# Two matmuls for each pair of weight halves instead of three: a 512-column moving tile, slabs of 256 columns

## The reference, cut to what matters

```python
proj = rms_norm(h) @ w_in              # 2048 x 9216, then attention, a 31-tap convolution, gates
y_attn = attention(q, k, v) @ w_attn_o # 1024 x 2048
y_conv = conv(...) @ w_conv_o          # 1024 x 2048
h = h + rms_norm(merged @ w_out)       # 2048 x 2048
gate, up = split(rms_norm(h) @ w_gate_up)  # 2048 x 11264
h = h + rms_norm((silu(gate) * up) @ w_down)   # 5632 x 2048
x @ ev_w_in                            # 2048 x 6144, then a second attention and a pooling
mixed @ ev_w_out                       # 2048 x 2048, then a layer norm
r, k, v, g = xr @ w_r, xk @ w_k, xv @ w_v, xg @ w_g   # 2048 x 2048 each
o = scan over the tokens of r, k, v, decay, a          # done in chunks of 64 tokens
(o * silu(g)) @ w_o                    # 2048 x 2048, then a layer norm
```

## Time and profile before

| | us |
|---|---|
| median of 3 runs (2875.58 to 2877.81) | 2876.98 |
| profiled execution, its own time | 2880.46 |
| its span in the trace | 2878.6 |
| mean granted TensorE clock, share of full | 0.945 |
| matmuls in the trace | 21760, of which 18240 are the stream's |
| DVE busy | 1599.9 |
| ACT busy | 1196.4 |

### The profile page before, as it was taken

One profiled execution on the slowest core, in us unless ns is written; L12 is line 12 of the kernel. 1 busy time (PEld: TensorE's weight loads), 2 busy tenths in 40 slices (PEclk: granted clock), 3 DMA queues, 4 the chain that ended last, 5 costly groups with the idle time before them and its releaser, 6 DMA issues.

```text
span 2878.6 us, 49871 instructions
## 1 busy us (share of the span) xinstructions
PE 2618.1 (91%) x21760; PEld 2543.9 (88%) x21760; DVE 1599.9 (56%) x2000; ACT 1196.4 (42%) x1458; POOL 72.9 (3%) x100
## 2 busy tenths in 40 slices
PE   7999999998999999999979999977857587999887
PEld 7999899997999999999979998976757587988787
DVE  5877676645555555544465655454367854243354
ACT  4333444434433433333334546355642243244433
POOL 0000000000000000000000000000011101011000
PEclk9999999999999999999999999999978797898889
DMA  6555455553555556555545564543324354121252
GB/s 218 184 169 155 139 175 163 170 188 112 182 183 183 177 180 193 179 182 179 180 132 182 158 182 140 160 146 114 98 74 139 101 172 139 52 67 60 83 180 97
DMA packets 115770, 429.44 MB, mean 149 GB/s; under 512 B 13328, under 2 KB 13328, under 8 KB 114592
## 3 DMA queue, kind: packets, MB, share of 16 engines
q1 hardware_dynamic: 111312, 404.59, 45.1%
q0 software_dynamic: 4240, 21.67, 2.3%
HBM read 415.72 MB, written 10.49 MB: 148 GB/s over the span
## 4 chain that ended last, share of the span: by engine, by line
PE 77%; DVE 11%; issue 5%; ACT 4%; DMA 2%; POOL 1%; SPq 0%; ACTq 0%; DVEq 0%; POOLq 0%
PE GP L1626 69%; PE SB L1626 8%; DVE wL L860 3%; ACT wH L428 2%; DVE T L860 1%; DVE Xs L1329 1%; DVE y L860 1%; PE SB L1630 1%; DVE x L860 0%; DVE acc L866 0%; DVE f L866 0%; DMA T<-t_blocks 0%; DMA raw<-w_in_dram 0%; DVE yL L860 0%; DMA gv<-g_keep 0%
## 5 line engine op out<-in xcount | busy, mean ns | idle before, releaser
L860 DVE TENSOR_TENSOR wL<-raw,wH 128x1024 fp32r<-128x1024 f32 x760 | 927.8, 1227 | 988.6 <-ACT wH L428 988.1
L428 ACT CAST wH<-raw 128x1024 fp32r<-128x1024 f32 x760 | 787.8, 1045 | 956.3 <-PE GP L1626 840.4
L1626 PE MATMUL GP<-yH,wL 128*128 128x256 f32 x1024 | 337.5, 330 | 81.0 <-DVE wL L860 59.2
L1626 PE MATMUL GP<-u2H,wL 128*128 128x256 f32 x1408 | 400.7, 285 | 7.5 <-DVE u2L L866 7.5
L1626 PE MATMUL GP<-u2L,wH 128*128 128x256 f32 x1408 | 399.5, 284 | 0.0
L1626 PE MATMUL GP<-u2H,wH 128*128 128x256 f32 x1408 | 399.4, 284 | 0.0
L1626 PE MATMUL GP<-uH,wL 128*128 128x256 f32 x1152 | 333.5, 290 | 15.9 <-DVE wL L860 15.9
L1626 PE MATMUL GP<-uH,wH 128*128 128x256 f32 x1152 | 328.5, 285 | 0.0
L1626 PE MATMUL GP<-uL,wH 128*128 128x256 f32 x1152 | 328.5, 285 | 0.0
L1626 PE MATMUL GP<-yL,wH 128*128 128x256 f32 x1024 | 308.4, 301 | 0.0
L1626 PE MATMUL GP<-yH,wH 128*128 128x256 f32 x1024 | 307.9, 301 | 0.0
(11 more groups left out here) (377 smaller groups left out, 5041.1 us busy)
## 6 DMA issues: line engine op xcount, KB each, us to landing
raw<-w_gate_up_dram SPq DMA_DIRECT2D x176, 512.0 KB, 4.1
raw<-w_in_dram SPq DMA_DIRECT2D x144, 512.0 KB, 3.7
raw<-ev_w_in_dram SPq DMA_DIRECT2D x96, 512.0 KB, 3.7
raw<-w_down_dram SPq DMA_DIRECT2D x88, 512.0 KB, 3.6
raw<-w_out_dram SPq DMA_DIRECT2D x32, 512.0 KB, 3.6
raw<-ev_w_out_dram SPq DMA_DIRECT2D x32, 512.0 KB, 3.6
raw<-w_k_dram SPq DMA_DIRECT2D x32, 512.0 KB, 3.6
raw<-w_r_dram SPq DMA_DIRECT2D x32, 512.0 KB, 3.6
```

Source lines behind the costliest of these rows:

```text
L428: e.copy(wH[SLOT[i]], h).then_inc(s["hi"], 1)
L860: return e.tensor_tensor(o, a, b, op)
L1626: return e.matmul(o, l, r, start=start, stop=stop, skip_group_check=True)
```

## The change

1. PE. H(x) and L(x) of one tile become one moving operand of 2 x 256 = 512 columns. For each row tile and column tile there are two matmuls where there were three: L(w) by 256 columns of H(x), and H(w) by 512 columns of H(x) and L(x).
2. PSUM. A column tile then fills a bank: 256 columns of what H(x) gives and 256 of what L(x) gives. A PSUM tile of two banks holds two column tiles, so a slab has 256 columns (184 slabs). To empty one, ACT copies the L(x) part to SBUF (`low`) and DVE adds the H(x) part (`high`); what was done while emptying (the factor rsU, a gate, a residual) is an operation of its own behind it.
3. Units. A unit is 512 rows by 256 columns: still 512 KB, 8 pairs of tiles, 760 units, the same number of columns through PE. It is loaded by two DMAs of 256 KB, each partition of each in two runs of 1 KB.
4. Order. Slabs go in pairs. In the first pair of most matrices, and in the first and the last pair of w_k, w_r and w_v, the units of the two slabs alternate (BY_TURNS), so that the moving tiles are needed no faster than before.
5. ACT's Sigmoid and Silu of gates, and the stores of v and g (POOL), go by 256 columns: twice as many, half as wide. w_v and w_g use two buffers in turn. post_stat, ln_sum and the norms' last parts go by 256 columns too. PLAN shifts a few steps by one or two units.

```diff
@@ tensor_program
-                for ku in range(kus):
-                    for k in range(2):
-                            for c in range(4):
-                                mm(ps[:, c, :], l, xh[:, kt, :], first_ and c % 2 == 0, False)
-                                mm(ps[:, c, :], h, xl[:, kt, :], False, False)
-                                ins = mm(ps[:, c, :], h, xh[:, kt, :], False, last_)
+                    for k in range(4):
+                        for c in range(2):
+                            mm(ps[:, c, 0, :], l, xb[:, 0, kt, :], kt == 0, False)
+                            ins = mm(ps[:, c], h, xb[:, :, kt, :], False, kt == 4 * KUS[name] - 1)
@@ sync_program
-                e.dma_start(raw[i % RAW], d[name][sl, ku]).then_inc(s[f"raw{i % RAW}"], 16)
+                cols = slice(256 * (sl % 2), 256 * (sl % 2) + 256)
+                for j in range(2):
+                    e.dma_start(raw[i % RAW][:, 512 * j:512 * j + 512].rearrange("p (k n) -> p k n", k=2),
+                                d[name][sl // 2, 2 * ku + j].rearrange("p (k n) -> p k n", k=2)[:, :, cols]).then_inc(s[f"raw{i % RAW}"], 16)
@@ scalar_program
+            def low(n, o):
+                e.wait_ge(s["unit"], END[n] + 1)
+                e.copy(o, two(n, 1)).then_inc(s["lh"], 1)
+            def empty_g(n, sl, j):
+                o = gv[:, 14:16, :] if j == 7 else kb[j % 2]
+                if j < 7:
+                    e.wait_ge(s[f"kb{j % 2}"], 64 + 16 * (j // 2))
+                low(n, o)
+                emptied(n)
+                e.activation(o, o, ACT.Silu).then_inc(s["kp"], 1)
@@ vector_program
+            def high(n, o):
+                e.wait_ge(s["lh"], n + 1)
+                tt(o, two(n, 0), o, ALU.add).then_inc(s["ev"], 1)
@@ vector_program, empty_in (empty_gu likewise)
-                tt(o_, ps, rep(rsU, 4), ALU.mult).then_inc(s["ev_dve"], 1)
+                high(n, o_)
+                emptied(n)
+                tt(o_, o_, rep(rsU, 2), ALU.mult).then_inc(s["val"], 1)
@@ vector_program, empty_r
-                tt(q, q, ps, ALU.mult).then_inc(s["ev_dve"], 1)
+                high(n, kb[j % 2])
+                emptied(n)
+                e.wait_ge(s["dec_d"], 14 * (j // 2) + 13)
+                q = rh[:, 2 * j:2 * j + 2, :]
+                tt(q, q, kb[j % 2], ALU.mult).then_inc(s["aw"], 1)
@@ order of the units
+        if _i // 2 in BY_TURNS.get(_n, ()):
+            UNITS += [(_m + h, k) for k in range(_kus) for h in range(2)]
+        else:
+            UNITS += [(_m + h, k) for h in range(2) for k in range(_kus)]
```

More of the change, by code:

```diff
@@ L841, in scalar_program @@
             stream("w_k", empty_k, mixed_tiles)
-            stream("w_r", idle)
-            stream("w_v", empty_keep("vk", ACT.Copy))
-            stream("w_g", empty_keep("gk", ACT.Silu), turn=turn)
+            stream("w_r", empty_r)
+            stream("w_v", empty_v)
+            stream("w_g", empty_g, turn=turn)
             for t in range(turn_at(U0["w_o"]), len(TURNS)):
@@ L1199, in centre @@
                     yield
+                yield
             def norm_head(key):
@@ L1684, in ready_in @@
+                    if behind and u - 2 in ENDS and ENDS[u - 2] >= first:
+                        behind(ENDS[u - 2] - first)
+                    side(u)
+                if behind:
+                    for n in (last - 2, last - 1):
+                        if END[n] > U1[name] - 3:
+                            behind(n - first)
             def ready_in(sem):
@@ L1701, in attention @@
             def attention(hh):
-                emptied(N0["w_in"] + (9 if hh else 6))
+                e.wait_ge(s["val"], 20 if hh else 14)
                 for tk in range(2):
@@ L2053, in tensor_program @@
-            stream("ev_w_in", xH, xL, ready_in("xl"))
+            stream("w_in", uB, ready_in("ul"))
+            stream("w_attn_o", oB, ready_heads)
+            stream("w_conv_o", cB, ready_in("c_l"))
+            stream("w_out", mB, ready_pairs("ml"), behind=post_stat(sq1, "p1"))
+            stream("w_gate_up", u2B, ready_in("u2l"))
+            stream("w_down", hB, ready_pairs("hl"), behind=post_stat(sq3, "p2"))
+            stream("ev_w_in", xB, ready_in("xl"))
             for _ in tasks["pool_mix"]:
@@ L2062, in tensor_program @@
+            stream("w_r", yB, ready_mix(1))
+            stream("w_v", yB, ready_mix(2))
+            e.wait_ge(s["aw"], 24)
             e.wait_ge(s["sv_dve"], 27)
-            emptied(N0["w_v"] + 3)
-            stream("w_g", yH, yL, ready_mix(3), turn=turn)
+            emptied(N0["w_v"] + 7)
+            stream("w_g", yB, ready_mix(3), turn=turn)
             for t in range(turn_at(U0["w_o"]), len(TURNS)):
                 turn(t)
-            stream("w_o", oyH, oyL, ready_gated, behind=ln_sum("l2", y2))
```

704 lines of the change are left out of this document (365 added, 339 removed).

## The result

The changed kernel takes **2903.42 us** (median of 4 runs, 2898.87 to 2906.0), beside 2877.39 for the kernel before on the same chip: a ratio of **1.0085, 95% interval 1.0064 to 1.0105**. It is slower by 0.9%; the forecast was 2822, the range 2768 to 2895. The profiled execution has a span of 2901.7 us, 23.1 more than before.

What follows compares the result with a forecast made beforehand. The prediction took PE's pace to bound most stages, and task chains mostly w_k to w_g. Its terms, -66 - 4 + 6 + 3 + 9 - 4 + 1, summed to -55 us, giving 2822 us for the median, range 2768 to 2895.

Steps and rivals of the forecast that it cites:

- part 2: Emptying slabs from PSUM: more work for DVE and ACT, taken as covered by PE (DVE 83% in w_in), 0 us.
- PE's columns and loads: Two matmuls per pair for three: -66 us in the PE-bound stages, -4 in w_v and part of w_k.
- Reading (a): The extra 13.3 ns belongs to each matmul and its weight load: pair 346.7 ns for 360, gain 13.3 ns.
- Columns: Rival: the extra time belongs to the columns, 512-column matmul 240 ns, no PE gain; 2890 us, chance 0.22.
- load: Rival: 120 ns is a weight load's time, 512-column matmul 216 ns, 24 ns gained per pair; 2769 us, chance 0.10.
- Half: Rival: only part of the extra time is saved, 6.7 ns per pair, 2857 us; chance 0.17.
- DVE and ACT become the bound: Rival: in w_in and ev_w_in, or alternating pairs stall; up to 20 us in w_in, 2855 us, chance 0.05.
- w_k to w_g, +18 - 4: Stages with DVE and ACT on the path: w_r +6, w_k +3, w_g +9 us; PE gain there -4.
- Ends of stages, -4: At w_out, w_down, ev_w_out and w_o the last slab, half the size, is emptied sooner: -4 us.
- The stage forecast at 493 us: w_gate_up was to last near 493 us for 521, with units of 2.77 us.
- Loads, +1: Loads in 1 KB packets stay hidden behind PE, costing only 1 us at the start.
- Loads become the bound: Rival: a 1 KB packet takes above 87 ns; at 94 ns, +80 us, 2960 us; chance 0.04.

Runs made afterwards that it cites:

- Experiment 1: Changed kernel with the 512-column matmul written as two of 256 columns, all else kept: 2953.08 us, ratio 1.0248 to the kernel before.
- 11: Changed kernel with w_in alone back to three 256-column matmuls and one emptying per slab: 2887.99 us, ratio 1.0035 to the kernel before.
- experiment 7: Kernel before with four extra 128x256 products on DVE behind each of w_in's 18 emptyings: 2887.91 us, ratio 1.0038.
- experiment 12: Kernel before with the steps of scale2 placed as the change has them, two behind unit 5 of w_gate_up: 2883.14 us, ratio 1.0018.
- experiment 9: Changed kernel with PE's last step of scale2 moved back behind unit 6 of w_gate_up: 2900.23 us, ratio 1.0074 to the kernel before.
- experiment 8: Kernel before with each unit loaded by two DMAs of 256 KB in runs of 1 KB: 2877.23 us, ratio 1.0001.
- L L H H: Changed kernel with both column tiles' L(w) matmuls first, then both H(w): 2906.46 us; the order was also used in later versions with five matrices back.

## Why the prediction was wrong

The direction was wrong, by part 2. Point by point, against the sum of -55:

- *PE's columns and loads, -66 and -4.* Reading (a) was right in kind: 347 ns a pair at full clock, 640 at half. Weighted by stage the pair took 352 ns in w_in and w_gate_up, 348 in w_down and 347 in ev_w_in. 1152 x 7.7 + 1408 x 7.7 + 704 x 12.3 + 768 x 13.1, with the small stages, is 50 us. Experiment 1's 50 is not the same sum: 12 of it are w_g's, and in w_in the gain went into waits. Mis-sized by 16 us, by the slower of two paces that no row of before shows. "Columns" and "load" fell: H(w)'s step, 230 ns at the fast pace and 237 at the slow one, is neither 240 nor 216. "Half" fell as a mechanism, since the fast pace has the whole gain; but its 6.7 ns a pair is just the slow pace, 353.3, and whether that is chance no run shows. The Trainium skill ("TensorE: Matmul & The Clock Gate", "Back-to-back issue gap") has N/2.4 + 2.5 ns, there for a matmul by itself; it does not fit this float32r stream here either: 116.7 and 230 measured, 109.2 and 215.8 by the page.
- *Emptying, 0.* **This is the step that failed**, and with it the sign. I took a mean share, 83% of DVE, for cover. The split of the weights has units of slack; the steps of the attention and of the second attention have none. `low` holds ACT for a unit of PE, the casts bunch behind it, DVE's next split waits for them, and the step that PE needs is behind that. From w_in to ev_w_out and in w_o the span rose by 8.5 us where the pairs gave 50: 58 us were lost, 31 of them in w_in and 11 in ev_w_in. In w_in the second emptying alone costs 18.4 us (experiment 1 against 11), and experiment 7 makes such a loss out of DVE's work alone. Not all of the 58 is the emptying: 5 in w_in belong to the new order, some 5 lie in the first seven units of w_gate_up, with the moved step, and ev_w_in's 11 and the rest no run isolates.
- *What a wait costs.* The prediction priced a late step at its own 0.5 to 1 us. In w_in PE stood 33.0 us for 13.9 before (the windows above and the earlier trace rows), 19 more. And of the 37.5 us at half clock PE was busy in 33.8, for 6.8 before; at half clock a pair takes 640 ns for 352, so 45% of these 27 us is lost, an estimate of 12. Together 31, which is what w_in lost. Over all the stages just named there are 65 us more at half clock (w_attn_o has 3.4 of them), of which PE was busy in 44: **some 20 of the 58 us**, beside 34 in which it stood. This third of the loss was in no term. The rows for it were there: the kernel before had half clock behind its longest waits too (the earlier trace rows is such a stretch).
- *The rival "DVE and ACT become the bound"* had the place right, 20 us in w_in, and lacked the clock; it ended at 2855 and had a chance of 0.05.
- *The moved step*, one unit for scale2, was read and priced at nothing ("PLAN shifts a few steps"): 5 us in experiment 12. In the new order the first seven units took the same 5 us more, but taking the step back gave 1.4 of them in experiment 9.
- *w_k to w_g, +18 - 4.* The four stages took 830.2 us for 816.2, as written ("some 830 us for 816"), but not by those parts: w_k +14.5 for +3, w_r +8.8 for +6, w_v -4.3, w_g -5.0 for +9. In w_r, where DVE was full, PE's wait for wL went from 44.0 to 35.9, and 27.7 us of waiting for a PSUM tile, until DVE had emptied it into stage or small, came beside it (below). In w_g the extra table loads cost nothing that can be seen; its -5.0 is within what the stage moves by itself.
- *Ends of stages, -4.* Not there: w_out and w_down gained 1.7 and 8.9 us, of which the pairs explain 3.4 and 8.7.
- *The stage forecast at 493 us.* w_gate_up took 516.6. The 493 does not follow from the prediction's own sum: 1408 pairs by 13.3 ns are 19 us, 502 for 521; it leaves out most of the waits at the first units.
- *Loads, +1.* Right, and better: w_in starts at 16.2 us for 16.0, experiment 8 finds nothing. "Loads become the bound" fell.

Sum: -50, +58, +14, with 1 for the rest, is +23, the difference of the spans.

Waits of PE in w_r, kernel after:

```profile
PE GP L1707 <- DVE wL L937: 35.9, 8, 6.8
PE GP L1707 <- DVE stage L937: 17.5, 2, 10.2
PE GP L1707 <- DVE small L937: 10.2, 1, 10.2
```

All three are for DVE, which is busy for 164 of 210 us there.

What stays open: what puts the stream into one pace or the other. It holds for a hundred units and more, changes where PE has other work between but also where it has none (unit 31 of w_gate_up), and is there with either order of the two matmuls; the four traces with L L H H are free of it. Also open is w_g, which took 307 to 320 us in versions that hardly differ there, with 82 to 112 us at half clock: in the kernel before 312.5, with loads in 1 KB runs 306.8. No run isolates it.

## What to carry to other kernels

A busy share is no cover for a step that PE waits for: follow the list of the engine that makes it, and ask what an added wait holds up behind it, one step at a time. Price a wait of TensorE at its own length plus what the granted clock loses behind it, which here added some 0.6 of it (w_in) to nearly as much again (experiment 7). A form that saves instructions on TensorE and pays on the vector engines belongs in the stages where they have nothing else to do: taken back in five matrices of thirteen, with the waits taken apart, the same change ran at 2870.5 us, 33 below the change as made and 0.16% below the kernel before. That is the best of the versions tried, and its interval ends at 0.9999: a gain over the kernel before is hardly shown.

## What the runs showed of the hardware that was not expected

- The same alternation of 256 and 512 columns of float32r ran at 346.7 or at 353.3 ns a pair, for tens of units to nearly a whole stage, at full clock; the doubled order at 348.4; three matmuls of 256 at exactly 360.
- In TensorE's longest waits the granted clock fell to 1.2 GHz: in the wait of 4.50 us for `sc` for 6.8 us, 1.3 of them before PE went on, in the one of 4.6 us for `sq` for 6.8, 2.7 of them before. From w_in to ev_w_out the kernel before had 34.7 us at half clock, the kernel after 96.1.
- Loads in runs of 1 KB: 415312 packets took 43.0 to 45.5% of the queue's engines, where 111312 had taken 45.1%. That is 48 to 50 ns a packet, close to what their bytes alone had cost before (the prediction's lower bound was 47).
